# Token columns of a decoder step's linear products, read and written in pairs from two halves

## The reference

```python
def _swiglu(h, w_in, w_out):
    gu = h @ w_in
    gate, up = gu[..., :D_FF], gu[..., D_FF:]
    return (jax.nn.silu(gate) * up) @ w_out

for i in range(DEPTH):                      # DEPTH = 2, D_MODEL = 1024, D_FF = 2816
    x = x + 0.5 * _swiglu(_rms_norm(x, ffn1_norm[i]), ffn1_w_in[i], ffn1_w_out[i])
    h = _rms_norm(x, mix_norm[i])
    y = gdn_mixer(h, ...) if i == 0 else stick_breaking_mixer(h, k_all, v_all, ...)
    x = x + y
    x = x + 0.5 * _swiglu(_rms_norm(x, ffn2_norm[i]), ffn2_w_in[i], ffn2_w_out[i])
    x = x + (p[i] @ ple_w_in[i]) * jax.nn.sigmoid(_rms_norm(x, ple_norm[i]) @ ple_w_gate[i])
    if i == 0:
        kv = _rms_norm(x, kv_norm) @ w_kv
y = _rms_norm(x, final_norm)
```

## Time and profile before

| what | us |
|---|---|
| median of 3 runs | 2749.09 |
| lowest and highest | 2748.33, 2750.84 |
| the profiled execution | 2749.38 |
| its span, first to last instruction | 2747.6 |
| PE busy | 2702.4 |
| DVE busy | 1327.1 |
| ACT busy | 921.6 |

### The profile page before, as it was taken

One profiled execution on the slowest core, in us unless ns is written; L12 is line 12 of the kernel. 1 busy time (PEld: TensorE's weight loads), 2 busy tenths in 40 slices (PEclk: granted clock), 3 DMA queues, 4 the chain that ended last, 5 costly groups with the idle time before them and its releaser, 6 DMA issues.

```text
span 2747.6 us, 52338 instructions
## 1 busy us (share of the span) xinstructions
PE 2702.4 (98%) x22041; PEld 2609.8 (95%) x22041; DVE 1327.1 (48%) x1715; ACT 921.6 (34%) x1384; POOL 292.2 (11%) x348
## 2 busy tenths in 40 slices
PE   8999999999999999999999999999999999999999
PEld 8999999998887999999999999999986699999999
DVE  4434347765555643333564343434547754343354
ACT  4222124454323332222342222212348732122243
POOL 2000002211224100000110000000133210000011
PEclk9999999999999999999999999999999999999999
DMA  5223222221012232323222332322303422232321
GB/s 141 77 80 88 77 80 88 87 82 30 20 34 76 83 92 77 92 77 89 84 78 85 121 113 77 92 77 84 105 18 108 142 74 84 82 86 78 87 92 54
DMA packets 308138, 225.96 MB, mean 82 GB/s; under 512 B 8270, under 2 KB 301567, under 8 KB 307967
## 3 DMA queue, kind: packets, MB, share of 16 engines
q1 hardware_dynamic: 307280, 224.26, 27.1%
q0 software_dynamic: 576, 0.00, 0.0%
q10 hardware_dynamic: 162, 0.04, 0.0%
HBM read 212.14 MB, written 12.13 MB: 82 GB/s over the span
## 4 chain that ended last, share of the span: by engine, by line
PE 95%; DVE 3%; issue 1%; ACT 1%; POOL 1%; DVEq 0%; POOLq 0%; ACTq 0%
PE ps L537 80%; PE ps L2445 1%; PE ps L556 1%; PE ps L2411 1%; PE ps L1810 1%; PE ps L2453 1%; PE ps L2350 1%; PE ps L1814 1%; PE ps L1558 0%; PE ps L2595 0%; PE ps L2447 0%; PE ps L2448 0%; DVE w_lo L489 0%; PE ps L1660 0%; PE ps L1833 0%
## 5 line engine op out<-in xcount | busy, mean ns | idle before, releaser
L537 PE MATMUL ps<-hx_hi,w_lo 128*128 128x320 f32 (+1 forms) x3730 | 1096.5, 294 | 0.0
L537 PE MATMUL ps<-hx_lo,w_hi 128*128 128x320 f32 (+1 forms) x3730 | 1096.0, 294 | 0.0
L537 PE MATMUL ps<-hx_hi,w_hi 128*128 128x320 f32 (+1 forms) x3730 | 1089.6, 292 | 1.6 <-DVE w_lo L489 1.3
L474 ACT ACTIVATE w_hi<-raw 128x1024 fp32r<-128x1024 f32 (+1 forms) x362 | 375.4, 1037 | 1216.9 <-PE ps L537 1216.2
L537 PEld LDWEIGHTS ps<-hx_hi,w_hi 128*128 128x128 f32 x3730 | 700.2, 188 | 4.7 <-DVE w_lo L489 2.5
L537 PEld LDWEIGHTS ps<-hx_hi,w_lo 128*128 128x128 f32 x3730 | 700.2, 188 | 0.0
L537 PEld LDWEIGHTS ps<-hx_lo,w_hi 128*128 128x128 f32 x3730 | 699.0, 187 | 0.3
L537 PE MATMUL ps<-hid_hi,w_hi 128*128 128x320 f32 (+1 forms) x1920 | 566.5, 295 | 2.2 <-DVE hid_lo L2239 0.5
L537 PE MATMUL ps<-hid_lo,w_hi 128*128 128x320 f32 (+1 forms) x1920 | 567.6, 296 | 0.0
L537 PE MATMUL ps<-hid_hi,w_lo 128*128 128x320 f32 (+1 forms) x1920 | 561.3, 292 | 0.0
L489 DVE TENSOR_TENSOR w_lo<-raw,w_hi 128x1024 fp32r<-128x1024 f32 (+1 forms) x362 | 460.9, 1273 | 108.7 <-ACT w_hi L474 108.6
(11 more groups left out here) (500 smaller groups left out, 2316.7 us busy)
## 6 DMA issues: line engine op xcount, KB each, us to landing
raw<-in_ffn_w_in SPq DMA_DIRECT2D x176, 512.0 KB, 5.0
raw<-in_ffn_w_out SPq DMA_DIRECT2D x64, 512.0 KB, 4.1
raw<-in_a_w_in SPq DMA_DIRECT2D x33, 512.0 KB, 4.6
raw<-in_ffn_w_out SPq DMA_DIRECT2D x32, 384.0 KB, 3.5
raw<-in_ple_w_gate SPq DMA_DIRECT2D x8, 1024.0 KB, 5.2
raw<-in_w_kv SPq DMA_DIRECT2D x16, 512.0 KB, 4.1
k_page<-in_cache_k SPq DMA_DIRECT2D x16, 512.0 KB, 3.6
v_page<-in_cache_v SPq DMA_DIRECT2D x14, 512.0 KB, 4.7
```

Source lines behind the costliest of these rows:

```text
L474: nc.scalar.activation(w_hi[:, m, 0:k], s.view(m, slot), ACT.Copy).then_inc(w_hi_done, 1)
L537: last = nc.tensor.matmul(TILE[m][:, c0:c1], w[:, m, k], h[:, k, c0:c1], start=k == 0 and a == 0, stop=k == k_all - 1 and a == 2)
```

## The change

A new helper, `woven`, views a row of columns as pairs of adjacent columns, taken alternately from the first and the second half of the row: columns 0 and 1, then 160 and 161, then 2 and 3, then 162 and 163, and so on (for the part of 256 columns the second half begins at 128). The matmuls of `multiply` and `multiply_pin` read their token columns through it and write PSUM through it, so that every column arrives where it was before. Number, order, size and operands of these matmuls stay the same.

The unread matmuls of `tail_products` are other ones: 80 instead of 60.

```diff
--- before.py
+++ after.py
@@ -226,6 +226,10 @@
 
         QUARTERS = (slice(0, P // 2), slice(P // 2, P))
         TOP, BOTTOM = QUARTERS
+
+        def woven(ap):
+
+            return ap.rearrange("p (two n pair) -> p n two pair", two=2, pair=2)
 
         def halves(ap):
             return ap.rearrange("p (c n) -> p c n", c=2)
@@ -534,7 +538,7 @@
                 middle = ((w_hi, lo), (w_lo, hi))[::1 if hi is hx_hi else -1]
                 for c0, c1 in PARTS:
                     for a, (w, h) in enumerate(((w_hi, hi), *middle)):
-                        last = nc.tensor.matmul(TILE[m][:, c0:c1], w[:, m, k], h[:, k, c0:c1],
+                        last = nc.tensor.matmul(woven(TILE[m][:, c0:c1]), w[:, m, k], woven(h[:, k, c0:c1]),
                                                 start=k == 0 and a == 0, stop=k == k_all - 1 and a == 2)
                 if between:
                     between(k)
@@ -553,7 +557,7 @@
             for k in range(PK):
                 for c0, c1 in PARTS:
                     for a, (w, h) in enumerate(((pw_hi, hi), (pw_hi, lo), (pw_lo, hi))):
-                        last = nc.tensor.matmul(PIN[:, c0:c1], w[:, m, k], h[:, k, c0:c1],
+                        last = nc.tensor.matmul(woven(PIN[:, c0:c1]), w[:, m, k], woven(h[:, k, c0:c1]),
                                                 start=k == 0 and a == 0, stop=k == PK - 1 and a == 2)
             last.then_inc(pin_done, 1)
@@ -2699,32 +2703,46 @@
             pe.wait_ge(y_left_ev[1], 2)
             mm, out, x = nc.tensor.matmul, ps[:, 6], hx_hi[:].rearrange("p k t -> p (k t)")
             w = w_hi[:, 0].rearrange("p k n -> p (k n)")
-            one = x[:, 0:1].to_broadcast((P, C0))
-            W = P // 2
-            for n in range(5):
-                mm(out[:, 0:C0], w[:, 0:P], x[:, 0:C0], start=True, stop=True)
-            for n in range(5):
-                mm(out[:, 0:C0], w[:, 0:P], x[:, 0:C0], start=False, stop=True, skip_group_check=True)
-            for n in range(5):
-                mm(out[:, 512 - C0:], w[:, 0:P], x[:, 0:C0], start=True, stop=True)
-            for n in range(5):
-                mm(out[:, 0:C0], w[:, 0:P], x[:, 8:C0 + 8], start=True, stop=True)
-            for n in range(5):
-                mm(out[:, 0:C0], w[:, 0:P], x[:, 16:C0 + 16], start=True, stop=True)
-            for n in range(5):
-                mm(out[:, 0:C0], w[:, 0:P], x[:, 24:C0 + 24], start=True, stop=True)
-            for n in range(5):
-                mm(out[:, 0:C0], w[:, 16:P + 16], x[:, 0:C0], start=True, stop=True)
-            for n in range(5):
-                mm(out[:, 0:C0], w[:, 0:P], one, start=True, stop=True)
-            for n in range(5):
-                mm(out[:, 0:512], w[:, 0:P], x[:, 0:512], start=True, stop=True)
-            for n in range(5):
-                mm(out[:, 0:T - C0], w[:, 0:P], x[:, 0:T - C0], start=True, stop=True)
-            for n in range(5):
-                mm(out[:, 0:C0], w[0:W, 0:P], x[0:W, 0:C0], start=True, stop=True)
-            for n in range(5):
-                mm(out[:, 0:C0], w[:, n % 2 * P:(n % 2 + 1) * P], x[:, T * (n % 2):T * (n % 2) + C0], start=True, stop=True)
+            to = out[:, 0:C0]
+            pairs = to.rearrange("p (two n q) -> p n two q", two=2, q=2)
+            for n in range(8):
+                mm(to, w[:, 0:P], x[:, 0:C0], start=True, stop=True)
+            for n in range(4):
+                mm(to, w[:, 0:P], x[:, 0:C0].rearrange("p (two n) -> p n two", two=2), start=True, stop=True)
+            for n in range(4):
+                mm(to, w[:, 0:P], x[:, 0:T].rearrange("p (two n) -> p n two", two=2)[:, 0:C0 // 2], start=True, stop=True)
+            for n in range(4):
+                mm(to, w[:, 0:P], x[:, 0:2 * T].rearrange("p (two n) -> p n two", two=2)[:, 0:C0 // 2], start=True, stop=True)
+            for n in range(4):
+                mm(to, w[:, 0:P], x[:, 0:8 * T].rearrange("p (two n) -> p n two", two=2)[:, 0:C0 // 2], start=True, stop=True)
+            for n in range(4):
+                mm(to, w[:, 0:P], x[:, 0:C0].rearrange("p (two n q) -> p n two q", two=2, q=2), start=True, stop=True)
+            for n in range(4):
+                mm(to, w[:, 0:P], x[:, 0:C0].rearrange("p (two n q) -> p n two q", two=2, q=4), start=True, stop=True)
+            for n in range(4):
+                mm(to, w[:, 0:P], x[:, 0:C0].rearrange("p (two n q) -> p n two q", two=2, q=8), start=True, stop=True)
+            for n in range(4):
+                mm(to, w[:, 0:P], x[:, 0:C0].rearrange("p (two n q) -> p n two q", two=2, q=16), start=True, stop=True)
+            for n in range(4):
+                mm(pairs, w[:, 0:P], x[:, 0:C0].rearrange("p (two n q) -> p n two q", two=2, q=2), start=True, stop=True)
+            for n in range(4):
+                mm(to, w[:, 0:P], x[:, 0:C0].rearrange("p (f n) -> p n f", f=4), start=True, stop=True)
+            for n in range(4):
+                mm(to, w[:, 0:P], x[:, 0:C0].rearrange("p (f n q) -> p n f q", f=4, q=2), start=True, stop=True)
+            for n in range(4):
+                mm(to, w[:, 0:P], x[:, 0:2 * C0].rearrange("p (n q) -> p n q", q=4)[:, :, 0:2], start=True, stop=True)
+            for n in range(4):
+                mm(out[:, 0:256], w[:, 0:P], x[:, 0:256], start=True, stop=True)
+            for n in range(4):
+                mm(out[:, 0:256], w[:, 0:P], x[:, 0:256].rearrange("p (two n) -> p n two", two=2), start=True, stop=True)
+            for n in range(4):
+                mm(out[:, 0:256], w[:, 0:P], x[:, 0:T].rearrange("p (two n) -> p n two", two=2)[:, C0 // 2:T // 2], start=True, stop=True)
+            for n in range(4):
+                mm(out, w[:, 0:P], x[:, 0:512], start=True, stop=True)
+            for n in range(4):
+                mm(out, w[:, 0:P], x[:, 0:512].rearrange("p (two n) -> p n two", two=2), start=True, stop=True)
+            for n in range(4):
+                mm(to, w[:, 0:P], x[:, 0:C0], start=True, stop=True)
```

## The result

The changed kernel took 3699.5 us (median of four runs, 3688.6 to 3712.4) against 2749.1 before: ratio 1.346, 95% interval 1.341 to 1.350. The profiled execution took 3702.0 us with a span of 3700.2. The forecast was 2756 with a range to 2900.

A forecast was written before the change was run, and what follows sets the result against it. The prediction took PE to bound the kernel (busy 98%), with one matmul line of the linear products 80% of the chain. From 2749.4 us, linear products 0 and tail +7.0 gave 2756.4, stated as 2756; range 2612 to 2900.

The forecast's parts named there:

- I take zero for the read and the write: Linear products: reading SBUF and writing PSUM in pairs adds 0 us; chance of unchanged linear products 0.33.
- the half-rate rival: Linear products: read or write cannot follow pairs at 2.4 GHz, matmuls take half-clock times; +1866 us, 4623 us, chance 0.21.
- dearer by the visit: Linear-product reads: pairs double the visits to stretches of memory, doubling the 8 ns cost; +133 us, 2889 us, chance 0.20.
- the 8 ns that a row loses: 320-column matmul at full clock: about 8 of 146 ns put down to reading different columns, against 138 for one repeated.
- The rival of a cheaper read: Linear-product reads: turns between two halves relieve the read; -133 us, 2623 us in full, 2690 for half; chance 0.26.
- The sixteen rows of L2325: Plain float32 matmuls reading runs of eight columns: taken as sixteen of 128 columns, 118 ns each, undisturbed by the broken path.
- The tail: Unread matmuls at the end: 3.0 us for 6528 more columns plus 4.0 us for single-column reads, +7.0 us, nothing hiding it.
- 120 ns more apiece: Tail: upper value, from half-clock rows, for each of 20 matmuls of 320 single columns read alternately; 0.12 us each.

## Why the prediction was wrong

**The bound was right.** PE's matmul line was the kernel, one nanosecond on each matmul was 17 us, and nothing hid the loss. Some 55 ns on each of 17142 matmuls give the 950 us.

**The step that failed was "I take zero for the read and the write".** For the write zero was right, measured at 0.04% with an interval that takes in no change (0.9993 to 1.0016). For the read the mean cost is some 55 ns per matmul: 60 at 320 columns and 51 at 256. The reason I gave, that a stream of pairs is near enough to a row since the loss at full rate is small, has the logic upside down. By the rule above, the loss of a row (13 of 146 ns) was the sign that the fetch of a group was already longer than the two steps in which a side uses it up, 1.76 ns against 1.67 (it gives 141 of the 146; the other 5 are not explained). What is at its limit for four columns of a group is far beyond it for two.

**The rows could have said more.** L2719 (one column repeated) and the half-clock rows together hinted at a fetch time: a row gets four columns in about 1.8 ns at full clock and loses nothing in 3.3 ns at half. With about that time for each visit of two columns, the half-rate rival follows with a mechanism. I had it as the case at the far end, at 0.21, and left it outside the range. The truth lies between the two rivals: 206 ns at 320 columns, where dearer by the visit had 155 and fetches at every visit would give 282. The rival "dearer by the visit" had the right sign and place, and its price was wrong: I doubled the 8 ns that a row loses, and the loss measured is 60 ns. Only the excess of the fetch over the clock shows in a row, and that says little about the price of a fetch; but doubling the whole fetch gives 282, too much.

**The rival of a cheaper read** was wrong for pairs, and right for the same idea one column finer. By the two sides, its condition, that turns between two halves relieve the fetch, is met when the two columns that go in together come from two halves: each side then has four columns from a group. With pairs both sides jump to and fro between the halves at every step.

**One row was misread.** The sixteen rows of L2325 are eight matmuls of the program, since plain float32 has two rows for a matmul (L2730). Its columns went in at half the rate that I took, so it said even less about this change; nothing in the sum came from it.

**The tail** was forecast at +7.0 us. The stretch from its first matmul to the end was 11.45 us before and is 14.05 now, +2.6. Three things were off. The single columns in turn cost nothing (L2711, L2713: 136 ns) where I had set 120 ns more apiece, though L2729, from four places, takes 170. And the stretch at half clock, which I had taken to stay in the tail, didn't fall there: the mean clock in it was 1.00 against 0.85. Dear shapes that I had not priced made up part of it: the pairs themselves (210 ns), pairs from four places (L2731: 1.11 us for four, 277 ns) and two of every four columns (L2733: 285 ns).

**On the page cited.** The Trainium skill's "Advanced Engine Details and Errata", section "Memory Cachelines", has SBUF lines of 16 bytes; the runs agree, by the group of four float32 and eight bf16 columns. That two hits on a line are enough is not so for TensorE at full clock: two of every four columns in fp32r take 282 ns against 146 for a row, every fourth column in bf16 282 against 136 to 140. For PSUM the stronger of its two sentences, that any non-contiguous pattern slows matmuls, isn't borne out for pairs: ratio 1.0004.

**What stays open.** Pairs in turn enter 80 groups on a side, as a row does, and take 206 ns; with a fetch at every jump it would be 282. The same middle shows in bf16 (pairs 170 ns, single columns in turn 302) and plain float32 (single columns in turn 339). So going back to a group left shortly before costs less than a new one and more than staying; these runs don't say by what. Four, eight and sixteen columns at a time, which never go back to a group, still take 152 ns where a row takes 146, and that doesn't shrink with the number of jumps. Single columns in turn from three places were not measured. The price of pairs, the change itself, is thus measured and placed in the read, but not derived. Nor do the runs say why the first long stretch of the changed kernel has 191 ns per matmul and the like one later 186.

## What to carry to other kernels

Where a matmul takes longer than its columns by the clock, look at the order in which it reads them. Here each new group of 16 bytes had a price in fixed time, and a shape slightly short of full rate (146 ns where the clock needs 133) was a warning: orders with shorter runs fell off steeply, to 206 and 282 ns. In fp32r, reading single columns in turn from two halves took 7% off a matmul of 320 columns. Unread matmuls at a program's end show such a price in one trace, for some 0.6 us a shape, before 17142 matmuls are bet on it. Where a tile is copied anyway, the copy can put the order right.

## What the runs showed of the hardware that was not expected

- Each newly entered group of 16 bytes of the token operand takes 1.76 ns (562 ns for 320 of them in bf16). In fp32r every second column takes as long at half clock as at full (11 and 12 matmuls in 2.80 us).
- At half clock reading in pairs costs nothing (0.27 us at 320 columns, 0.21 at 256, as a row).
- fp32r behaves as if two sides fetched its columns, the first and the second of each two (every fourth column: 290 ns, as every second), bf16 and plain float32 as if one did (every eighth and every fourth column: 562 ns).
- A plain row in fp32r is not at TensorE's full rate: 146 ns at 320 columns, against 136 for the same columns in turn from two halves and for a bf16 row.
- Writing PSUM in pairs to two places costs nothing (381.56 us for 2910 matmuls either way), and VectorE reads every second column of PSUM at no loss (757 ns for 576, 758 for adjacent ones).
